# Latent attention heads of a streaming encoder: scores over 128 rows, reordered latent blocks, and probabilities scaled on GpSimd

## What is computed

```python
q_lat, kv_lat, k_pe = split(h @ w_in, [384, 256 + 384])        # 384, 256 and 32 columns
q  = (rms_norm(q_lat, q_norm) @ w_q_up).reshape(b, s, 16, 64 + 32)
q_pe = apply_rope(q[..., 64:], cos, sin)
kv = (rms_norm(kv_lat, kv_norm) @ w_kv_up).reshape(b, s, 16, 64 + 64)
k_pe = apply_rope(k_pe, cos, sin)                              # one for all heads
for i in range(4):                                             # 128 queries each
    logits = (q_nope @ k_nope.T + q_pe @ k_pe.T) * 96 ** -0.5  # keys 0 to (i + 1) * 128
    logits = where(chunk(key) <= chunk(query), logits, -inf)   # chunks of 64
    out_i = softmax(logits) @ v
y = out @ w_out
```

## Time and profile before

| What | Value |
|---|---|
| median of 3 runs | 1857.47 us (1857.16 to 1858.07) |
| the profiled execution | 1857.64 us |
| its span, first to last instruction | 1855.8 us |
| mean granted TensorE clock | 0.996 of full speed |
| PE busy | 98% of the span |
| DVE busy | 50% |
| ACT busy | 34% |
| GpSimd busy | 9% |
| latent blocks, key/value blocks | about 1246 to 1309 us |
| 16 heads and the begun output blocks | about 1309 to 1440 us |
| rest of the output projection | about 1440 to 1479 us |

### The profile page before, as it was taken

How to read it: one execution, slowest core, us unless ns; L and a number is a source line. 1 busy time by engine, 2 the same in 40 slices (tenths; PEclk the granted TensorE clock), 3 DMA queues, 4 the chain that set the end, 5 groups by cost and what they waited for, 6 DMA issues and landing times.

```text
span 1855.8 us, 23429 instructions
## 1 busy us (share of the span) xinstructions
PE 1813.1 (98%) x8601; PEld 1482.5 (80%) x8601; DVE 929.2 (50%) x1422; ACT 623.3 (34%) x1044; POOL 169.8 (9%) x140
## 2 busy tenths in 40 slices
PE   7999999999999999999999999999999899999998
PEld 5888888878788888888888888888666788888886
DVE  5433433568654334345543443457897544344344
ACT  5422222336543223223322221243465442132222
POOL 0100100022011001010110110100111011010010
PEclk9999999999999999999999999999999999999998
DMA  6333333232233333323333333232011333333321
GB/s 177 103 102 91 97 96 96 85 107 76 84 92 95 98 97 96 102 82 99 102 91 101 92 100 94 84 102 73 23 37 57 91 91 102 93 100 102 91 80 56
DMA packets 321552, 168.89 MB, mean 91 GB/s; under 512 B 13329, under 2 KB 317646, under 8 KB 321486
## 3 DMA queue, kind: packets, MB, share of 16 engines
q1 hardware_dynamic: 321136, 167.21, 31.1%
q10 hardware_dynamic: 350, 0.83, 0.1%
HBM read 162.50 MB, written 2.10 MB: 89 GB/s over the span
## 4 chain that ended last, share of the span: by engine, by line
PE 65%; issue 23%; DVE 8%; DMA 1%; POOL 1%; ACT 1%; SPq 1%; POOLq 0%; DVEq 0%; ACTq 0%
PE bank L1069 21%; PE bank L1071 21%; PE bank L1070 21%; DVE sm L1002 1%; POOL work L453 1%; DVE work L1017 1%; DVE work L928 1%; SPq L385 1%; DMA r_kv<-work 1%; DVE xg L979 1%; DVE work L978 1%; DVE sm L1007 1%; DVE w_lo L705 0%; DMA work<-x 0%; DVE bank L997 0%
## 5 line engine op out<-in xcount | busy, mean ns | idle before, releaser
L1069 PE MATMUL bank<-h_hi,w_hi 128*128 128x512 f32 x1536 | 601.1, 391 | 1.7 <-issue 1.7
L1071 PE MATMUL bank<-h_hi,w_lo 128*128 128x512 f32 x1536 | 598.3, 390 | 0.0
L1070 PE MATMUL bank<-h_lo,w_hi 128*128 128x512 f32 x1536 | 598.1, 389 | 0.0
L705 DVE TENSOR_TENSOR w_lo<-w_raw,w_hi 128x1024 fp32r<-128x1024 f32 (+2 forms) x320 | 394.9, 1234 | 314.8 <-ACT w_hi L517 304.4
L517 ACT ACTIVATE w_hi<-w_raw 128x1024 fp32r<-128x1024 f32 (+2 forms) x320 | 319.5, 998 | 296.1 <-PE bank L1071 296.0
L1069 PEld LDWEIGHTS bank<-h_hi,w_hi 128*128 128x128 f32 x1536 | 288.8, 188 | 61.8 <-issue 2.2
L1071 PEld LDWEIGHTS bank<-h_hi,w_lo 128*128 128x128 f32 x1536 | 288.6, 188 | 60.3
L1070 PEld LDWEIGHTS bank<-h_lo,w_hi 128*128 128x128 f32 x1536 | 288.9, 188 | 58.9
L1069 PE MATMUL bank<-y_hi,w_hi 128*128 128x512 f32 x832 | 326.3, 392 | 5.8 <-DVE w_lo L705 5.1
L1071 PE MATMUL bank<-y_hi,w_lo 128*128 128x512 f32 x832 | 325.3, 391 | 0.0
L1070 PE MATMUL bank<-y_lo,w_hi 128*128 128x512 f32 x832 | 324.9, 391 | 0.0
(11 more groups left out here) (137 smaller groups left out, 1009.3 us busy)
## 6 DMA issues: line engine op xcount, KB each, us to landing
w_raw<-ffn_gu SPq DMA_DIRECT2D x176, 512.0 KB, 3.8
w_raw<-ffn_d SPq DMA_DIRECT2D x64, 512.0 KB, 3.7
w_raw<-ffn_d SPq DMA_DIRECT2D x32, 384.0 KB, 3.3
w_raw<-a_in SPq DMA_DIRECT2D x10, 512.0 KB, 4.0
w_raw<-a_out SPq DMA_DIRECT2D x8, 512.0 KB, 3.7
w_raw<-b_out SPq DMA_DIRECT2D x8, 512.0 KB, 3.6
w_raw<-b_in SPq DMA_DIRECT2D x5, 512.0 KB, 4.0
w_raw<-b_qup SPq DMA_DIRECT2D x16, 144.0 KB, 2.3
```

The lines of the kernel that those rows point to most:

```text
L705: last = v.tensor_tensor(w_lo[:, sl, 0:k, 0:m], w_raw[:, sl, 0:k, 0:m], w_hi[:, sl, 0:k, 0:m].bitcast(F32), ALU.subtract)
L1069: t.matmul(b[:, :], wh, hi[:, c, :], start=c == 0, stop=False)
L1070: t.matmul(b[:, :], wh, lo[:, c, :], start=False, stop=False)
L1071: last = t.matmul(b[:, :], wl, hi[:, c, :], start=False, stop=c == k - 1)
```

## The change

- `LAT` puts the latent blocks in another order: two key/value chunks, the position key, three query chunks. The statistic of the key/value chunks is now the second of the three, with its sum inside the position key's block and its spread inside the block after it; its values are kept in a tile of their own, s_kv, for ACT. The sum over the query chunks stands inside the first key/value block, its spread behind the second.
- The rows 96 to 127 of kt hold the position key too. A score is then a product over 128 rows: 64 unrotated ones, 32 with the cosine part and 32 with the sine part of the query. `scaled_q` is one instruction on 128 rows, and the addition on GpSimd for each head is gone. SP issues four copies into kt in place of two, now ahead of the load of the third key/value block.
- DVE makes only the reciprocals of a head (two sets of them, by h % 2); GpSimd multiplies the probabilities, four `tensor_scalar` instructions for each head, in place.
- The first query block is written to bank 2, the second to bank 0 with two blocks of distance.
- ACT evacuates a pair's output ahead of the transposed tiles of head h-1. Behind the last head, the split of out_b+3 stands ahead of the last pair's evacuation on ACT and DVE, and PE finishes chunks 6 and 7 of a block together.

```diff
-    out += ffn + [(KD, P)] * 5 + [(KD, QD)] + [(KKV, KV_COLS)] * KV_BLOCKS + ...
+    out += ffn + [(KD, P)] * KKV + [(KD, QD)] + [(KD, P)] * KQ + [(KKV, KV_COLS)] * KV_BLOCKS + ...
+LAT = (KQ, KQ + 1, None, 0, 1, 2)
+M_Q = M_B + 2
...
-    out += two(6) + [(0, 1)] * (KV_BLOCKS + HEADS + 1) + late(KD + FFN_BLOCKS - KD)[1:] + two(KD)
+    out += two(6) + [(0, 1)] * KV_BLOCKS + [(2, 4), (0, 2)] + [(0, 1)] * (HEADS - 1) + late(...)[1:] + two(KD)
...
 # SP
             for g in range(KV_BLOCKS):
+                if g == 2:
+                    sp.wait_ge(rot_done, R_B + 1)
+                    for e in range(2):
+                        for half in range(2):
+                            sp.dma_start(kt_b[e][HD + half * ROPE_B:HD + (half + 1) * ROPE_B, :, :],
+                                         k_pe[HD:QD, :].unsqueeze(1).to_broadcast([ROPE_B, PAIRS, S])
+                                         ).then_inc(kpe_in, 16)
                 load(n + g, 0, cols(b_kvup[0], g * KV_COLS, KV_COLS))
...
-                if h == 3:
-                    sp.wait_ge(rot_done, R_B + 1)
-                    for e in range(2):
-                        sp.dma_start(kt_b[e][HD:QD, :, :], ...).then_inc(kpe_in, 16)
...
 # GpSimd
             for h in range(HEADS):
-                pool.wait_ge(evac_done, n + h + FIRST + 1)
-                g.tensor_tensor(qt_b[pr, h % 2, :], qt_b[pr, h % 2, :], xg[pr, h % 2, :],
-                                ALU.add).then_inc(rot_done, 1)
+                for bk, tiles in enumerate(S_BANKS):
+                    pool.wait_ge(brec, 3 * h + bk + 1)
+                    if h or bk:
+                        pool.wait_ge(p_ready, 2 * PAIRS + 3 * h + bk)
+                    for i in tiles:
+                        pv = p_b[h % 2][:, P_AT[i]:P_AT[i] + (i + 1) * P]
+                        last = g.tensor_scalar(pv, pv, sm[:, h % 2, 3, i:i + 1], None, ALU.mult)
+                    last.then_inc(p_ready, 1)
...
 # ACT, heads
                 exponentials(h)
+                if h >= 4 and h % 2 == 0:
+                    head_pair_out(PAIRS + h // 2 - 2)
                 if h > 0:
                     transposed(h - 1)
-                if h >= 4 and h % 2 == 0:
-                    head_pair_out(PAIRS + h // 2 - 2)
+            head_pair_out(2 * PAIRS - 2)
             transposed(HEADS - 1)
-            for p in range(PAIRS - 2, PAIRS):
-                head_pair_out(PAIRS + p)
-            n = square(n + HEADS, G_FFN2 + KD)
+            high(n + HEADS + AHEAD)
+            head_pair_out(2 * PAIRS - 1)
+            n = square(n + HEADS, G_FFN2 + KD, 1)
...
 # DVE, latent blocks
-            latent(0)
-            for k in range(1, KQ):
-                latent(k)
-            rms_values(M_B, KQ * P)
-            latent(KQ)
-            rms_spread(M_B + 1, m_q)
-            latent(4)
-            with_table(m_q, m_q, 1)
-            with_table(r_kv, r_x, 2)
-            low(n + 5 + AHEAD)
+            latent(0, 0)
+            latent(1, 1)
+            with_table(r_kv, r_x, 1)
+            low(n + 2 + AHEAD)
...
-            rms_values(M_B + 2, KKV * P, between=position_key)
+            rms_values(M_B, KKV * P, between=position_key)
+            v.tensor_copy(s_kv[:, :], st[:, 5, :]).then_inc(skv_ready, 1)
+            latent(3, 2)
+            rms_spread(M_B + 1, r_kv)
+            latent(4, 3)
+            latent(5, 4)
...
-                v.tensor_tensor(qt_b[0:QD, h % 2, :], b[0:QD, :], m_q[0:QD, :], ALU.mult)
-                v.tensor_tensor(xg[pr, h % 2, :], b[QD:P, :], m_q[QD:P, :], ALU.mult).then_inc(evac_done, 1)
+                v.tensor_tensor(qt_b[:, h % 2, :], b[:, :], m_q[:, :], ALU.mult).then_inc(evac_done, 1)
...
-                    v.reciprocal(sm[:, 0, 3, c], sm[:, 0, 2, c]).then_inc(brec, 1)
-                    dve.wait_ge(brec, 3 * h + bk + 1)
-                    for i in tiles:
-                        pv = p_b[h % 2][:, P_AT[i]:P_AT[i] + (i + 1) * P]
-                        last = v.tensor_scalar(pv, pv, sm[:, 0, 3, i:i + 1], None, ALU.mult)
-                    last.then_inc(p_ready, 1)
+                    if h > 1:
+                        dve.wait_ge(p_ready, 2 * PAIRS + 3 * (h - 2) + bk + 1)
+                    v.reciprocal(sm[:, h % 2, 3, c], sm[:, 0, 2, c]).then_inc(brec, 1)
...
             for g in range(KV_BLOCKS):
-                if g:
-                    low(n + g + AHEAD)
+                low(n + g + AHEAD)
                 scaled_k(g)
+                if g == 0:
+                    rms_values(M_Q, KQ * P)
+                if g == 1:
+                    rms_spread(M_Q + 1, m_q)
+                    with_table(m_q, m_q, 2)
...
-            for p in range(PAIRS - 2, PAIRS):
-                pair_out(PAIRS + p)
-            n = square(n + HEADS, 1.0, G_FFN2 + KD)
+            pair_out(2 * PAIRS - 2)
+            low(n + HEADS + AHEAD)
+            pair_out(2 * PAIRS - 1)
+            n = square(n + HEADS, 1.0, G_FFN2 + KD, begun=1)
...
 # PE
-            normed(n, 2)
-            normed(n, 3, lambda: sums(M_B, KQ), 6)
-            normed(n, 4, lambda: spread(M_B + 1))
-            normed(n, 5, lambda: sums(M_B + 2, KKV), 6)
+            normed(n, 2, lambda: sums(M_B, KKV), 6)
+            normed(n, 3, lambda: spread(M_B + 1))
+            normed(n, 4)
+            normed(n, 5)
...
                                         qt_b[:, h % 2, i * P:(i + 1) * P],
                                         kt_b[h % 2][:, h // 2, 0:(i + 1) * P], start=True, stop=True)
...
                 if g == 0:
-                    spread(M_B + 3)
+                    sums(M_Q, KQ)
                 values(n, g, 1)
+                if g == 1:
+                    spread(M_Q + 1)
...
             for j in range(4):
-                out_part(out_b + j, PAIRS, 6, 7)
-            for j in range(4):
-                out_part(out_b + j, PAIRS, 7, 8)
+                out_part(out_b + j, PAIRS, 6, 8)
```

More of the change, by code:

```diff
@@ L120, in rings @@
     out = four(FFN_BLOCKS) + two(2 + PAIRS + KD) + four(2 * FFN_BLOCKS)
-    out += two(6) + [(0, 1)] * (KV_BLOCKS + HEADS + 1) + late(KD + FFN_BLOCKS - KD)[1:] + two(KD)
+    out += two(6) + [(0, 1)] * KV_BLOCKS + [(2, 4), (0, 2)] + [(0, 1)] * (HEADS - 1) + late(KD + FFN_BLOCKS - KD)[1:] + two(KD)
     assert len(out) == len(BLOCKS)
@@ L399, in _ @@
             n = ffn(n, ffn1_gu[1], ffn1_d[1])
-            for j in range(5):
-                load(n + j, 0, cols(b_in[0], j * P, P))
-            load(n + 5, 0, cols(b_in[0], 5 * P - HD, QD))
+            for j, chunk in enumerate(LAT):
+                if chunk is None:
+                    load(n + j, 0, cols(b_in[0], 5 * P - HD, QD))
+                else:
+                    load(n + j, 0, cols(b_in[0], chunk * P, P))
             n += 6
             for g in range(KV_BLOCKS):
+                if g == 2:
[5 more added lines that the diff above has]
+                                         ).then_inc(kpe_in, 16)
                 load(n + g, 0, cols(b_kvup[0], g * KV_COLS, KV_COLS))
@@ L480, in _ @@
             power(M_B)
-            power(M_B + 2)
             pr = slice(HD, QD)
+            pool.wait_ge(pow_done, 6)
+            pool.wait_ge(evac_done, n + 2 + FIRST + 1)
+            g.tensor_tensor(k_pe[pr, :], k_pe[pr, :], xg[pr, 0, :], ALU.add).then_inc(rot_done, 1)
+            pool.wait_ge(rot_done, R_B + 1)
+            power(M_Q)
+            n += 6 + KV_BLOCKS + HEADS
             pool.wait_ge(pow_done, 7)
-            pool.wait_ge(evac_done, n + 5 + FIRST + 1)
-            g.tensor_tensor(k_pe[pr, :], k_pe[pr, :], xg[pr, 0, :], ALU.add).then_inc(rot_done, 1)
-            n += 6 + KV_BLOCKS
             for h in range(HEADS):
-                pool.wait_ge(evac_done, n + h + FIRST + 1)
-                g.tensor_tensor(qt_b[pr, h % 2, :], qt_b[pr, h % 2, :], xg[pr, h % 2, :],
-                                ALU.add).then_inc(rot_done, 1)
-            n += HEADS
+                for bk, tiles in enumerate(S_BANKS):
[6 more added lines that the diff above has]
+                    last.then_inc(p_ready, 1)
+            pool.wait_ge(p_ready, 2 * PAIRS + 3 * HEADS)
             power(M_F)
@@ L617, in _ @@
             n = ffn(n, G_MIX + KD)
-            for k in range(6):
+            at = 0
+            for k, chunk in enumerate(LAT):
                 high(n + k + AHEAD)
-                if k < KQ + KKV:
-                    gained_high(lat_hi[:, k, :], lt[:, k % 2, :], G_Q + k, n + k, k in (0, KQ))
+                if chunk is not None:
+                    gained_high(lat_hi[:, chunk, :], lt[:, at % 2, :], G_Q + chunk, n + k, chunk in (0, KQ))
+                    at += 1
             n += 6
-            act.wait_ge(nstep, 4 * STAT_KV)
+            act.wait_ge(skv_ready, 1)
             for g in range(KV_BLOCKS):
@@ L637, in _ @@
                                             VB[g % 2][half][:, i * KV_HEADS * HD:(i + 1) * KV_HEADS * HD],
-                                            ACT.Copy, scale=st[:, 5, tile:tile + 1])
```

(11 more changed lines are left out.)

35 lines of the change are left out of this document (17 added, 18 removed).

## The result

The changed kernel takes 1844.93 us (median of 4 runs, 1843.35 to 1845.75) against 1857.32 us (1856.63 to 1858.07): ratio 0.9931, 95% interval 0.9918 to 0.9943, 12.4 us less. The forecast was 1841.4, 16.1 less; the median lies inside the stated range of 1837 to 1850, but just outside the 1838 to 1844 that had the 0.67. A second set of runs gave 1844.05 us, ratio 0.9921 (0.9908 to 0.9934).

A forecast was written before the change was run, and what follows sets the result against it. PE, busy 98% of the span, was taken as the bound. Gains of 0.7 (front), 7.0 (heads), 0.5 (low-part wait) and 7.9 (end) make 16.1 us: 1857.5 to 1841.4 us, range 1837 to 1850.

The forecast's parts named there:

- PE's 6.73 us a head: Latent heads: PE needs 13.47 us for two heads without its idle time; six such pairs make 80.8 us.
- DVE relieved by 2.16 us a head: Latent heads: multiplications (1.46) and the 32-row product (0.70) leave DVE; its cycle falls from 6.8 to about 4.6 us.
- the six waits: Latent heads: PE's waits for the pair's low part, 6.6 us in all, go with ACT's pair output ahead.
- GpSimd's 3.7 us: Latent heads: the four multiplications of a head on GpSimd take 3.7 us, bounds 1.46 and 5.2.
- the 1 us of slack: Latent heads: GpSimd ends 9.0 us after a head's scores start, PE wants the probabilities at 10.0 to 10.4.
- only heads 0 to 2 have no outputs in between: s(2) at +11.6: First heads: scores of head 2 start 11.6 us after those of head 0, before 11.0.
- The front: Stretch ahead of the heads: 0.7 us gained up to head 0's scores; 2.1 if copies cost nothing, -1.5 if waits double.
- The end: Behind the heads: two weight waits shortened and half-speed matmuls gone, 7.9 us; one more low-part wait gone, 0.5.
- FFN stages are the same code: Behind the output projection: FFN stages unchanged, only started 16 us earlier.
- A: Rival, heads: GpSimd and DVE block each other at the shared port, the loop gives nothing, 1848.5 us; chance 0.17.
- B: Rival, heads: GpSimd itself paces them and the kernel is slower, 1872 us at 8.7 us a head; chance 0.07.
- C: Rival, front: copies hold the weights, PE idles over 2 us; 4 us lost, not 0.7 won, 1846 us; chance 0.09.

The follow-up runs named there:

- Experiments 2: Changed kernel with the multiplication of the probabilities back on DVE: 1841.4 us beside 1844.05 for the changed kernel.
- experiment 5: Kernel before with only the 128-row scores, one scaling instruction a head and no GpSimd addition: 1846.82 us against 1858.03, ratio 0.9940.
- experiment 4: Changed kernel with the four copies into kt moved ahead of the first query block's load: 1844.66 us beside 1844.05.
- experiment 8: Changed kernel with the multiplication back on DVE and the copies into kt ahead of the first query block: 1840.38 us.
- experiment 6: Kernel before with only the multiplication moved to GpSimd, which keeps its addition for each head: 1854.85 us against 1858.03, ratio 0.9988.
- experiment 11: Kernel with multiplication on DVE and later copies, with PE asking for one statistics sum and two spreads later: 1837.3 us beside 1840.4.
- Experiment 7: Changed kernel with one more 512-column GpSimd multiplication a head: 1849.96 us against 1844.05 for the changed kernel, timed in another batch.

## Why the prediction was right, and where not

**PE's 6.73 us a head.** Right to 0.1 us in twelve heads (82.15 against 80.8 + 1.4). Reading PE's groups out of two heads and striking its one wait gave the new period, whatever relieved DVE.

**DVE relieved by 2.16 us a head.** Right in size, wrong in credit. The part-by-part sum put both edits into one term and never asked what 0.70 us alone would do: 6.8 - 0.70 = 6.1, with half a pair output 6.45, under 6.73. With the prediction's own 0.5 for waits between the stages it is 6.95, just above, so this sum alone would not have settled it; the runs did. Experiments 2 and 5 show that this edit carries the loop and that, on top of it, the multiplication's move only adds its latency. The prediction also had ACT's new order end the six waits; in experiment 5 they are gone with the old order.

**GpSimd's 3.7 us.** Mis-sized. It answers to rows 6:

```profile
L502 POOL TENSOR_SCALAR work<-work,sm 128x512 f32<-128x512 f32 x16 | 25.0, 1562 | 2.7 <-POOL work L502 2.7
L502 POOL TENSOR_SCALAR work<-work,sm 128x384 f32<-128x384 f32 x16 | 19.9, 1244 | 0.0
L502 POOL TENSOR_SCALAR work<-work,sm 128x256 f32<-128x256 f32 x16 | 14.8, 923 | 2.7 <-POOL work L502 2.7
L502 POOL TENSOR_SCALAR work<-work,sm 128x128 f32<-128x128 f32 x16 | 9.7, 603 | 55.2 <-DVE sm L1031 55.2
```

1.56 + 1.24 + 0.92 + 0.60 = 4.33 us, with two hand-overs between banks of 0.17 us 4.64 from first start to last end (1320.30 to 1324.94), within the bounds of 1.46 and 5.2. The estimate by the Trainium skill (GPSIMD Engine Reference, sections 3.1 and 4.1), 1.9 us, is not borne out; the measurement decides. It started at s+4.9 and not s+5.3, so the hand-over came at s+9.5 instead of s+9.0, within the 1 us of slack, and heads 3 to 15 never saw it.

**The first heads.** Here the step "only heads 0 to 2 have no outputs in between: s(2) at +11.6" failed; it came at +13.7. 0.5 us is the later hand-over. The other 1.6 is the clock: I had priced the wait and not what follows it. It is the largest miss of the sum. An idle time of 1.58 us had been followed by full speed, and from that I took short waits as harmless; three waits of 0.22, 0.43 and 1.29 us within 3 us were followed by half speed, in both executions of the changed kernel and in experiment 4. In experiment 8, without them, full speed stays; in experiment 6 it stays with them. What decides between the two is open.

**The front.** 1.0 us for the 0.7 of the sum. The named waits were there, all smaller: 0.42 us for the running sum (forecast 0.6), 0.85 for the diagonal (1.0), 0.32 for sum M_Q (0.6), none at key block 2 (0.5). By the prediction's own terms the key blocks end at 1309.5 and not 1309.7, which makes its 0.7 about 0.95. That this is so close to the measured 1.0 is in part luck: the four idle times were 1.1 us less in all than forecast, and each wait costs more than its idle time, since it breaks the overlap of matmuls too (0.26 us each in experiment 11). The lock between GpSimd and DVE is there as in rows 6:

```profile
1265.53 1.05 PE L1102 MATMUL bank<-ones,acc 128*128 128x1 f32 x8 [0.42 <-DVE acc L741]
1269.55 0.16 DVE L766 TENSOR_TENSOR st<-st 128x4 f32<-128x4 f32 x1
1269.66 1.29 POOL L490 TENSOR_TENSOR work<-work,xg 32x512 f32<-32x512 f32 x1 [1.17 <-DVE xg L982]
1269.74 1.23 DVE L768 TENSOR_TENSOR st<-st 128x4 f32<-128x4 f32 x1
1272.34 1.16 PE L1113 MATMUL bank<-diag,ones 128*128 128x128 f32 x8 [0.85 <-DVE diag L776]
```

The copies' transfers ran at 150 to 200 GB/s; a copy landed 8.4 us after its issue (median), the key/value loads 8.3 instead of 3.6, and ACT stood 4.1 us for the third block's weights. Experiment 4 prices it for PE: 0.8 us, where the prediction had 1.4 (2.1 without the copies, 0.7 with them).

**The end.** 8.3 us won where 8.4 were said (the S(15) wait included); of it 0.8 is given back at the last FFN's norm, which the prediction had at nothing ("FFN stages are the same code"). PE reaches the spread before DVE has the diagonal. The first two rows are the kernel before, the others the changed one:

```profile
1485.59 1.23 DVE L705 TENSOR_TENSOR w_lo<-w_raw,w_hi 128x1024 fp32r<-128x1024 f32 x1 [1.16 <-ACT w_hi L517]
1486.76 0.16 DVE L745 TENSOR_SCALAR st<-bank 128x4 f32<-128x4 f32 x1
...
1473.01 0.95 PE L1102 MATMUL bank<-ones,acc 128*128 128x1 f32 x8
1473.91 1.22 DVE L721 TENSOR_TENSOR w_lo<-w_raw,w_hi 128x1024 fp32r<-128x1024 f32 x1 [1.16 <-ACT w_hi L529]
1475.05 0.15 DVE L761 TENSOR_SCALAR st<-bank 128x4 f32<-128x4 f32 x1
...
1477.22 0.88 DVE L776 TENSOR_SCALAR diag<-cst,st 128x128 f32<-128x128 f32 x4
1478.15 1.16 PE L1113 MATMUL bank<-diag,ones 128*128 128x128 f32 x8 [0.63 <-DVE diag L776]
```

DVE's split of a weight block (L705, now L721) starts 28.8 us after B4 in both traces. PE's sum started 28.95 us after B4 and now starts 27.87 after it, since the slow clock behind B4 is gone. So DVE takes up the sum (L745, now L761) behind the split, 2.04 us after the sum's start instead of 0.98, and the diagonal is late by that. Experiment 11 removes the wait and gains 0.7.

**The rivals.** A (the shared port paces the heads) did not come: the reciprocals took 0.15 us and L1023, once L1007, 0.15 with one column and 0.28 on average with two (0.35 before). At worst it took 0.59 where a GpSimd instruction ran, so single ones passed the 0.3 that was to be A's sign, and the average did not:

```profile
1409.24 0.92 POOL L502 TENSOR_SCALAR work<-work,sm 128x256 f32<-128x256 f32 x1 [0.17 <-POOL work L502]
1410.33 1.56 POOL L502 TENSOR_SCALAR work<-work,sm 128x512 f32<-128x512 f32 x1 [0.17 <-POOL work L502]
...
1410.45 0.59 DVE L1023 TENSOR_SCALAR sm<-sm 128x2 f32<-128x2 f32 x1
```

So the rule of the Trainium skill (SBUF — State Buffer, Practical consequences) fits the lock, and its price here is some 0.1 us a head on an engine that waits anyway. A's price had a slip of its own: 5.5 us and four waits of 0.5 are 7.5 us a head, not 7.3. B did not come either: its sign, PE idle ahead of the transposes for GpSimd, stood in head 0 alone. Experiment 7 shows its slope: 1.6 us more of GpSimd a head cost 5.9 us by the medians and 4.8 by the trace. C did not come. The sum fell short by 3.7 us against the median: 2.1 at S(2), 0.8 at the norm, and the rest with the front's 0.3 the other way is within what the unchanged stretch ahead differs from execution to execution.

## What to carry to other kernels

When one engine paces a loop, take the paced engine's own period first and ask for each edit alone whether it gets the pacing engine below it; whatever is moved beyond that point buys nothing and can cost its latency where the loop starts. Price a wait of PE with what the clock did behind such waits in the traces at hand, and keep it as a range: three such waits were followed by half speed in three executions and by full speed in another kernel's. And when a stage gets shorter, look for the next place where PE asks for a result that used to be ready (a statistic, a diagonal): asking one or two chunks later cost nothing here.

## What the runs showed of the hardware that I had not expected

- A GpSimd tensor_scalar with one tensor input and a scalar for each row took 1.56 us for 128x512 float32, longer than its tensor_tensor with two inputs (1.29 us). By the four shapes it is 2.5 ns a column and 0.28 us of its own, (1562 - 603) / 384. DVE's took 0.49 us for 512 columns.
- Copies that write 32 rows each kept the DMA engines about as busy as weight loads did and moved little more than half as much. Four of 512 KB kept the queue busy from 1272 to 1284 us, and weight loads behind them in SP's queue landed 4.7 us later than usual. A stretch of the copies and the next one, of the loads behind them (the last two figures are the DMA engines' share and GB/s):

```profile
1282.00:1284.00 2.00, 2.00 (x10) 1.67 (x9) 2.00 (x3) 1.07 (x2) 0.00 (x0) 1.00 0.92 187
1284.00:1286.00 2.00, 2.00 (x10) 1.67 (x9) 0.32 (x1) 0.00 (x0) 0.00 (x0) 1.00 0.98 322
```

- PE's granted clock fell to its lower level behind three short waits, none over 1.3 us (0.83 from 1320 to 1330 us), and stayed at 1.00 behind three waits of 0.69, 0.46 and 1.29 us in experiment 6. In the first mixer it fell behind the same code in some executions and not in others (1.00, 0.83, 0.66 between 410 and 420 us).
